# Two layers of a hybrid decoder trunk: a triangular inverse begun in 16x16 blocks on GpSimd, and the rotary row exchange done by transfers

## The reference, cut to what matters

```python
def rope(x, pos):                    # x1, x2: the two halves of a head's 64 channels
    return jnp.concatenate([x1 * cos - x2 * sin, x2 * cos + x1 * sin], -1).astype(x.dtype)

def delta_rule_scan(r, w, k, v, kk, a):
    def step(S, inp):
        r_t, w_t, k_t, v_t, kk_t, a_t = inp
        sa = jnp.einsum('bhvk,bhk->bhv', S, -kk_t)
        S = S * w_t[:, :, None, :] + sa[..., None] * (kk_t * a_t)[:, :, None, :] + v_t[..., None] * k_t[:, :, None, :]
        return S, jnp.einsum('bhvk,bhk->bhv', S, r_t)
```

## Time and profile before

| | |
|---|---|
| time, median of 3 runs | 1683.96 us (1683.74 to 1685.42) |
| the profiled execution, span from first to last instruction | 1682.6 us |
| PE (TensorE) busy | 1656.3 us, 98% |
| DVE (VectorE) busy | 1273.1 us, 76% |
| ACT (ScalarE) busy | 1001.9 us, 60% |
| POOL (GpSimd) busy | 2.9 us, 0% |
| traffic of HBM over the span | 244 GB/s |

### The profile page before, as it was taken

How to read it: one execution, slowest core, us unless ns; L and a number is a source line. 1 busy time by engine, 2 the same in 40 slices (tenths; PEclk the granted TensorE clock), 3 DMA queues, 4 the chain that set the end, 5 groups by cost and what they waited for, 6 DMA issues and landing times.

```text
span 1682.6 us, 27509 instructions
## 1 busy us (share of the span) xinstructions
PE 1656.3 (98%) x10650; PEld 1402.5 (83%) x10650; DVE 1273.1 (76%) x1226; ACT 1001.9 (60%) x968; POOL 2.9 (0%) x12
## 2 busy tenths in 40 slices
PE   9999999999999999999999999999999999999997
PEld 8988788778887998978888888888888888888885
DVE  5766775664446668496478899898988889898987
ACT  6554463454444645444446777777776777777775
POOL 0000000000000000000000000000000000000000
PEclk9999999999999999999998999999999999999999
DMA  9433333556564543334376999999999999998993
GB/s 295 137 116 126 125 126 101 204 166 199 175 199 150 188 144 109 113 125 127 101 255 236 364 353 384 325 373 330 393 336 373 364 335 394 328 367 322 392 374 143
DMA packets 216185, 411.04 MB, mean 244 GB/s; under 512 B 9376, under 2 KB 83488, under 8 KB 215584
## 3 DMA queue, kind: packets, MB, share of 16 engines
q1 hardware_dynamic: 213840, 400.97, 67.5%
q10 hardware_dynamic: 2256, 8.82, 1.4%
HBM read 407.66 MB, written 2.10 MB: 244 GB/s over the span
## 4 chain that ended last, share of the span: by engine, by line
PE 93%; DVE 4%; issue 1%; ACT 1%; DMA 0%; SPq 0%; DVEq 0%; ACTq 0%
PE W L503 20%; PE W L505 19%; PE W L504 19%; PE Y L503 7%; PE Y L504 7%; PE Y L505 7%; PE Y L796 4%; PE W L701 1%; DVE w_lo L1801 1%; PE Y L701 1%; PE Y L783 1%; PE E L708 0%; DMA raw<-w_in 0%; PE Y L1072 0%; PE Y L1073 0%
## 5 line engine op out<-in xcount | busy, mean ns | idle before, releaser
L503 PE MATMUL W<-w_lo,x_hi 128*128 128x512 f32 (+1 forms) x1168 | 452.8, 388 | 1.5 <-DVE x_lo L2115 0.9
L505 PE MATMUL W<-w_hi,x_hi 128*128 128x512 f32 (+1 forms) x1168 | 442.2, 379 | 0.0
L504 PE MATMUL W<-w_hi,x_lo 128*128 128x512 f32 (+1 forms) x1168 | 441.5, 378 | 0.0
L1801 DVE TENSOR_TENSOR w_lo<-raw,w_hi 128x2048 fp32r<-128x2048 f32 x112 | 256.5, 2291 | 174.0 <-ACT w_hi L1292 172.7
L1808 DVE TENSOR_TENSOR w_lo<-raw,w_hi 128x2048 fp32r<-128x2048 f32 x144 | 329.6, 2289 | 45.6 <-ACT w_hi L1298 45.6
L1298 ACT ACTIVATE w_hi<-raw 128x2048 fp32r<-128x2048 f32 x144 | 276.1, 1917 | 72.6 <-PE Y L505 40.0
L1808 DVE TENSOR_TENSOR w_lo<-raw_more,w_hi 128x2048 fp32r<-128x2048 f32 x120 | 275.0, 2291 | 28.3 <-ACT w_hi L1298 27.6
L1298 ACT ACTIVATE w_hi<-raw_more 128x2048 fp32r<-128x2048 f32 x120 | 230.5, 1921 | 64.8 <-PE W L505 42.0
L1292 ACT ACTIVATE w_hi<-raw 128x2048 fp32r<-128x2048 f32 x112 | 214.2, 1913 | 81.6 <-PE W L505 47.8
L503 PEld LDWEIGHTS W<-w_lo,x_hi 128*128 128x128 f32 x1168 | 219.9, 188 | 45.0 <-issue 4.5
L505 PEld LDWEIGHTS W<-w_hi,x_hi 128*128 128x128 f32 x1168 | 219.7, 188 | 42.0
(11 more groups left out here) (332 smaller groups left out, 1853.3 us busy)
## 6 DMA issues: line engine op xcount, KB each, us to landing
raw<-w_in SPq DMA_DIRECT2D x123, 512.0 KB, 4.6
raw<-moe_gate SPq DMA_DIRECT2D x48, 1024.0 KB, 6.4
raw<-moe_up SPq DMA_DIRECT2D x48, 1024.0 KB, 7.0
...
```

Source lines behind the costliest of these rows:

```text
L503: nc.tensor.matmul(out_ap, lhs[0], rhs[1], start=start, stop=False)
L504: nc.tensor.matmul(out_ap, lhs[1], rhs[0], start=False, stop=False)
L505: return nc.tensor.matmul(out_ap, lhs[0], rhs[0], start=False, stop=stop)
L1801: V.tensor_tensor(w_lo[u % 3][:], raw[u % 3][:], w_hi[u % 3][:].bitcast(F32), ALU.subtract)\
```

## The change

The first four levels (0 to 3) of the inverse are no longer doubled on PE. The 64x64 blocks hold 64 diagonal blocks of 16x16 per pass, and each is inverted by itself. `pick` (DVE) multiplies `ac` by a mask and sums it into `diag` (128x8x16). `solve` (GpSimd) then moves `diag` to HBM (1024 runs of 64 bytes), loads it with one 16x16 matrix in each of 64 partitions (64 runs of 1 KB), runs 14 rank-one updates of two instructions each and one `memset`, stores the result (64 runs) and loads it back in rows as `solved` (1024 runs). Each step waits for the one before. `place` (DVE) spreads `solved` into `xt`. Levels 4, 5 and 6 stay as they were. The rotary exchange is done by `swap` (GpSimd): four transfers of 32 partitions (64 KB each) per `rope`, SBUF to SBUF, and the sign is put into the sine table once. The steps move in `TIMELINE`: in the first pass levels 4 to 6 and all of `cg`, `cu`, `cy`, `mean`, `scaled` stand one unit later than before, in the second pass `invert` half a unit later and level 4 earlier, and ropes 0 and 1 stand one unit earlier, rope 3 half a unit. `scores` of the second pass stands one unit later.

```diff
+BASE = 4
+BS, NB = 1 << BASE, HD >> BASE
+NM = 8 * 2 * NB
+STEPS = TOP - BASE + 1
+SOLVED = 2 * (BS - 2) + 2
...
-    ("masks", 0), ("front", "conv", 2), ("back", "conv", 2), ("invert", 0), ("shift", 3),
-    ("front", "conv", 3), ("mx", 0, 1), ("back", "conv", 3), ("dx", 0, 1), ("lora_w", 1), ("rate_w", 1), ("shift", 4),
-    ("front", "conv", 4), ("mx", 0, 2), ("back", "conv", 4), ("dx", 0, 2), ("lora_a", 1), ("rate_a", 1), ("ksq", 1),
-    ("decay", 1),
-    ("front", "conv", 5), ("mx", 0, 3), ("exps", 1), ("back", "conv", 5), ("dx", 0, 3), ("ss", 1), ("knorm", 1), ("shift", 5),
-    ("front", "gate0", 0), ("mx", 0, 4), ("back", "gate0", 0), ("dx", 0, 4), ("spread", 1), ("kk", 1), ("conv", 0),
-    ("front", "gate0", 1), ("mx", 0, 5), ("back", "gate0", 1), ("dx", 0, 5), ("conv", 1),
-    ("front", "gate0", 2), ("mx", 0, 6), ("osplit", 0, 0), ("osplit", 0, 1), ("back", "gate0", 2), ("dx", 0, 6), ("prep", 1),
...
-    ("front", "qkv", 3), ("scaled", 0), ("bonus", 1), ("back", "qkv", 3), ("rope", 0), ("scores", 1, 0),
-    ("front", "qkv", 4), ("scores", 1, 1), ("compact", 1), ("back", "qkv", 4), ("rope", 1),
-    ("front", "qkv", 5), ("rope", 2), ("back", "qkv", 5),
-    ("front", "branch0", 0), ("rope", 3), ("back", "branch0", 0), ("att_scores", 0),
+    ("pick", 0), ("front", "conv", 2), ("back", "conv", 2), ("shift", 3),
+    ("front", "conv", 3), ("back", "conv", 3), ("lora_w", 1), ("rate_w", 1), ("shift", 4),
+    ("front", "conv", 4), ("back", "conv", 4), ("lora_a", 1), ("rate_a", 1), ("ksq", 1), ("decay", 1),
+    ("front", "conv", 5), ("exps", 1), ("back", "conv", 5), ("ss", 1), ("knorm", 1), ("shift", 5),
+    ("front", "gate0", 0), ("place", 0), ("back", "gate0", 0), ("invert", 0), ("spread", 1), ("kk", 1), ("conv", 0),
+    ("front", "gate0", 1), ("mx", 0, 4), ("back", "gate0", 1), ("dx", 0, 4), ("conv", 1),
+    ("front", "gate0", 2), ("mx", 0, 5), ("osplit", 0, 0), ("osplit", 0, 1), ("back", "gate0", 2), ("dx", 0, 5), ("prep", 1),
+    ("front", "gate0", 3), ("mx", 0, 6), ("back", "gate0", 3), ("dx", 0, 6),
+    ("front", "qkv", 0), ("cg", 0, 0), ("back", "qkv", 0), ("cu", 0, 0),
+    ("front", "qkv", 1), ("cy", 0, 0), ("back", "qkv", 1), ("cg", 0, 1),
+    ("front", "qkv", 2), ("cu", 0, 1), ("back", "qkv", 2), ("cy", 0, 1), ("yrow", 0), ("decayed", 1), ("rope", 0),
+    ("front", "qkv", 3), ("mean", 0), ("back", "qkv", 3), ("var", 0), ("tok", 1), ("rope", 1),
+    ("front", "qkv", 4), ("scaled", 0), ("bonus", 1), ("back", "qkv", 4), ("scores", 1, 0),
+    ("front", "qkv", 5), ("scores", 1, 1), ("compact", 1), ("rope", 2), ("back", "qkv", 5), ("rope", 3),
+    ("front", "branch0", 0), ("back", "branch0", 0), ("att_scores", 0),
...
-    ("front", "gate1", 2), ("att_out", 0), ("back", "gate1", 2), ("att_out", 1), ("masks", 1),
-    ("front", "gate1", 3), ("invert", 1), ("mx", 1, 1), ("dx", 1, 1), ("back", "gate1", 3), ("mx", 1, 2), ("dx", 1, 2),
-    ("front", "branch1", 0), ("mx", 1, 3), ("dx", 1, 3), ("back", "branch1", 0), ("mx", 1, 4), ("dx", 1, 4),
-    ("front", "branch1", 1), ("mx", 1, 5), ("dx", 1, 5), ("mx", 1, 6), ("dx", 1, 6),
+    ("front", "gate1", 2), ("att_out", 0), ("back", "gate1", 2), ("att_out", 1),
+    ("front", "gate1", 3), ("place", 1), ("back", "gate1", 3), ("invert", 1), ("mx", 1, 4),
+    ("front", "branch1", 0), ("dx", 1, 4), ("back", "branch1", 0), ("mx", 1, 5), ("dx", 1, 5),
+    ("front", "branch1", 1), ("mx", 1, 6), ("dx", 1, 6),
...
+        blocks_in, blocks_out = (nc.dram_tensor(name, (8, P, BS), F32, kind="Internal").ap() for name in ("blocks_in", "blocks_out"))
...
+        own_blocks = cm[:, 1, :]
+        def by_row(ap):
+            return ap.rearrange("u j t -> j u t")
+        def by_block(ap):
+            return ap.rearrange("u (b j) t -> (u b) (j t)", j=BS)
...
+        SWAPPED = (t4[:], t1[:], t2[:], fin2)
+        QUARTERS = [slice(a, a + HD // 2) for a in range(0, P, HD // 2)]
...
-            def rope(l, s):
-                wait_jobs(pe, l * MIX_JOBS + JOB0["qkv"] + s + 1)
-                if s:
-                    pe.wait_ge(sem("rope_ready"), 4 * l + s)
-                else:
-                    pe.wait_ge(sem("tok_ready"), 2 * l + 2)
-                nc.tensor.matmul(E[:], rot, share[:, 2 * s:2 * s + 2, :].rearrange("p m t -> p (m t)"),
-                                 start=True, stop=True).then_inc(sem("rot_done"), 1)
...
+            def moved(n, leg):
+                pool.wait_ge(sem("blocks_moved"), 16 * (4 * n + leg))
+            def solve(l, p):
+                n = 2 * l + p
+                made = SOLVED * n + 1
+                pool.wait_ge(sem("blocks_made"), made)
+                pool.dma_start(by_row(blocks_in), diag[:]).then_inc(sem("blocks_moved"), 16)
+                moved(n, 1)
+                pool.dma_start(own[:].rearrange("p j t -> p (j t)"), by_block(blocks_in)).then_inc(sem("blocks_moved"), 16)
+                moved(n, 2)
+                for m in range(1, BS - 1):
+                    rest = BS - 1 - m
+                    grown = step[:, 0:m, 0:rest]
+                    nc.gpsimd.tensor_tensor(grown, own[:, 0:m, m].unsqueeze(2).to_broadcast([NM, m, rest]),
+                                            own[:, m, m + 1:BS].unsqueeze(1).to_broadcast([NM, m, rest]), ALU.mult)\
+                        .then_inc(sem("blocks_made"), 1)
+                    pool.wait_ge(sem("blocks_made"), made + 2 * m - 1)
+                    nc.gpsimd.tensor_tensor(own[:, 0:m, m + 1:BS], own[:, 0:m, m + 1:BS], grown, ALU.add)\
+                        .then_inc(sem("blocks_made"), 1)
+                    pool.wait_ge(sem("blocks_made"), made + 2 * m)
+                nc.gpsimd.memset(own[:].rearrange("p j t -> p (j t)")[:, ::BS + 1], 1.0).then_inc(sem("blocks_made"), 1)
+                pool.wait_ge(sem("blocks_made"), SOLVED * (n + 1))
+                pool.dma_start(by_block(blocks_out), own[:].rearrange("p j t -> p (j t)")).then_inc(sem("blocks_moved"), 16)
+                moved(n, 3)
+                pool.dma_start(solved[:], by_row(blocks_out)).then_inc(sem("blocks_moved"), 16)
+            def swap(l, s):
+                wait_jobs(pool, l * MIX_JOBS + JOB0["qkv"] + s + 1)
+                if s == 3:
+                    pool.wait_ge(sem("var_done"), 2 * l + 1)
+                elif s:
+                    pool.wait_ge(sem("decayed_ready"), 2 * l + 2)
+                else:
+                    pool.wait_ge(sem("prep_ready"), 2 * l + 2)
+                for i, to in enumerate(QUARTERS):
+                    pool.dma_start(SWAPPED[s][to], share[QUARTERS[i ^ 1], 2 * s:2 * s + 2, :]).then_inc(sem("swapped"), 16)
+                pool.wait_ge(sem("swapped"), 64 * (4 * l + s + 1))
+            for l in range(L):
+                solve(l, 0)
+                corner(l, 0)
+                for s in range(4):
+                    swap(l, s)
+                solve(l, 1)
+                corner(l, 1)
...
+            def pick(l, p):
+                n = 2 * l + p
+                if n == 0:
+                    for v, other in ((1, 0), (1, 2), (1, 3), (1, TOP)):
+                        link(V.tensor_tensor(own_blocks, cm[:, v, :], cm[:, other, :], ALU.add))
                 dve.wait_ge(sem("ac_ready"), n + 1)
+                picked = t3[:].rearrange("p m (u t) -> p (m u) t", t=HD)
+                link(V.tensor_tensor(picked, ac[:], own_blocks.unsqueeze(1).to_broadcast([P, 8, HD]), ALU.mult))
+                V.reduce_sum(diag[:], picked.rearrange("p u (b t) -> p u t b", b=NB), AX.X).then_inc(sem("blocks_made"), 1)
+            def place(l, p):
+                n = 2 * l + p
                 for c in range(NT):
+                    link(mask_level(BASE, c))
+                dve.wait_ge(sem("blocks_moved"), 16 * (4 * n + 4))
+                blocks = own_blocks.rearrange("p (b t) -> p b t", b=NB).unsqueeze(1).to_broadcast([P, 4, NB, BS])
                 for c in range(NT):
                     mine = slice(4 * c, 4 * c + 4)
+                    mark(V.tensor_tensor(xt[:, mine, 0, :].rearrange("p u (b t) -> p u b t", b=NB),
+                                         solved[:, mine, :].unsqueeze(2).to_broadcast([P, 4, NB, BS]), blocks, ALU.mult),
+                         "xt_ready", 2 * (STEPS + 1) * n + c + 1)
...
-                dve.wait_ge(sem("rot_done"), 4 * l + s + 1)
-                V.tensor_tensor(t4[:], tiles(E[:]), sin, ALU.mult)
+                other = SWAPPED[s]
+                if l == 0 and s == 0:
+                    dve.wait_ge(sem("cst_full"), 96)
+                    for quarter in QUARTERS[0::2]:
+                        last = V.tensor_scalar(cst[quarter, C_SIN:C_END], cst[quarter, C_SIN:C_END], -1.0, None, ALU.mult)
+                    link(last)
+                dve.wait_ge(sem("swapped"), 64 * (4 * l + s + 1))
+                V.tensor_tensor(other, other, sin, ALU.mult)
                 link(V.tensor_tensor(src, src, cos, ALU.mult))
-                mark(V.tensor_tensor(src, t4[:], src, ALU.add), "rope_ready", 4 * l + s + 1)
```

(37 more changed lines are left out.)

26 lines of the change are left out of this document (11 added, 15 removed).

## The result

The changed kernel takes 1671.9 us (median of 4 runs, 1671.4 to 1673.2) beside 1683.9 for the kernel before on the same chip: ratio 0.9928, 95% interval 0.9917 to 0.9940. The gain is 12.0 us where I forecast 32.3. The profiled execution has a span of 1669.6 us.

The account below looks back on a forecast made before the run. PE's instruction stream was taken as the bound. Sparing PE matmuls and waits gains 49.3 us, less 2.0 for first-pass waits and 15.0 for second-pass stops: 32.3 off 1684.0, forecast 1652 us, range 1636 to 1676 for 8 in 10.

Parts of the forecast that it names:

- The number of matmuls: On PE: 1152 fewer rows of 64x64, and no 128x512 rows into `E` from `share`.
- C: Chain from `pick` to `place`: four transfers at 2.7 us, 29 GpSimd instructions at 0.36, 21 us; bounds 13 and 40.
- rival (a): The chain stops PE in the second pass only, C from 16 to 26 us; 1640 to 1662 us; chance 0.50.
- The cover there: Second pass, from `pick`'s end until PE wants the result at `invert`: 15.0 us, so C is 6.0 us longer.
- 1.5 us of clock for a stop: PE's rows run at half clock after idling: 1.5 us added to each stop of more than 2 us.
- The ropes' 9.3 us: Rope matmuls taken off PE: 0.9 us a rope, 3.6 a layer; plus 2.1 us of waits for rope 3.
- Rival (c): The chain outlasts both passes' covers, C of 27 to 31 us; 1674 us at C = 29; chance 0.16.
- the fight between the engines: GpSimd stands still for 5 to 7 us of DVE's `w_lo` and `o_lo`, second cover: about 1665 us; about one in three.
- The lower price in the prediction: The Trainium skill's estimate for a GpSimd transfer of 64 KB: 2.15 us, making the time some 4 us less.
- place behind w_lo: First pass on DVE: `w_lo` starts 2.9 us into PE's unit, so PE waits 1.0 us at `invert`, twice 2.0.
- the 0.8 us at the scores: PE's four waits for the scores, 0.8 us, should go because no rope stands between the two steps of scores.
- rival (b): The chain fits its covers, C of 15 us or less: 47.3 us less, 1637 us; chance 0.18.

Follow-up runs that it names:

- keep_clock: The changed kernel with 20 matmuls of zeros put into PE's stop before `invert` of the second pass: 1668.8 us, ratio 0.9911.
- pe_ropes: The changed kernel with the four ropes of a layer on TensorE again, at the new places or within half a unit: 1681.2 us, ratio 0.9982.
- quiet_chain: The changed kernel with `w_lo` of gate1's last unit moved on DVE behind `place` of the second pass: 1669.6 us, ratio 0.9916.
- no_chain: The changed kernel without the whole of `solve`, so `place` multiplies zeros and the output differs: 1646.2 us, ratio 0.9784.
- late_low: The changed kernel with one number different: `w_lo` stands in the back half of qkv 4 on DVE instead of qkv 3: 1671.0 us, ratio 0.9918.
- transfers_only: The changed kernel without the 28 `tensor_tensor` instructions of `solve`, transfers and `memset` kept, so the output differs: 1645.4 us, ratio 0.9775.

## Why the prediction fell short

**What was right.** The number of matmuls, and that the chain would stop PE in the second pass. C of 24.9 us is inside rival (a), but (a) had PE stop in the second pass only, and its prices give 1659.5 us for this C; the other 12 us are the second and third point below. The cover there: PE wants the result at 235.7, 15.15 us after `pick`, less the 0.57 from `place` to PE 14.6; I had 15.0. The first: 25.8, I had 26.5. 1.5 us of clock for a stop, near the 1.1 and 1.4 of keep_clock. The ropes' 9.3 us agree with pe_ropes in size only, and that is partly luck, since 2.1 of them were another wait. Rival (c) named the fight between the engines, and it is there, at 1.9 us and not 5 to 7: of the three `w_lo` inside the second cover two ran while GpSimd issued its transfers or waited for them, and the `o_lo` at 230.66, with one input from PSUM, held no row.

**The step that failed first: C.** "I take 2.7" a transfer and 0.36 an instruction gave 21 us; it is 24.9 and 25.1 in the second pass, 29.6 and 30.0 in the first. An undisturbed instruction with its gap takes 0.35, so this price held; 1.9 us are the one row held by `w_lo` (quiet_chain), 2.1 the transfers. "DMA is busy for 35 to 39% here, so it is nearest the first" took an average over 67 us: three of the first pass's four transfers ran beside shares of 0.47 to 0.75. The lower price in the prediction, 2.15 us a transfer, was nearly met once in four (2.23), in the stop itself. The second stop became 10.3 and 10.5 us instead of 6.0: 8.8 us lost in the two layers.

**The second: place behind w_lo.** "In the trace it starts 2.9 us after PE begins this unit" took a distance between two engines from the old order, where PE still had level 3 to do over ACT's run. I had subtracted these matmuls from PE and let ACT and DVE come forward with it. It is 3.0 without the chain (no_chain) and 3.84 and 4.16 with it: 6.0 us lost, and the clock behind it, for which I had put nothing. In no_chain the first pass's stop of 3.0 us is followed by half the clock in layer 0 and not in layer 1, and from the first scores to the second layer 0 takes 1.6 us longer (115.8 against 114.2), so I estimate some 3 us for two stops.

**The third: a wait that I didn't look for.** I took out the 0.8 us at the scores and put nothing in. `scaled` had moved one unit on, the number that lets `w_lo` stand behind it had not, and PE waits 1.8 us in each layer: 3.6. By late_low that number is the cause of this wait, but most of the lateness comes back at the attention scores, so it was to be had back only in small part.

**The sum.** 32.3 - 8.8 - 6.0 - 3 - 3.6 = 10.9 beside 12.0 measured. The 3 is an estimate, the other terms are PE's waits. The floor closes as well: 47.3 of rival (b), less 4.0 for the first pass (3.0 instead of 1.0, twice), 3.6 for the scores and some 3 for the clock, is 36.7; no_chain gained 37.1.

**What stays open.** The same 3.0-us stop lost the clock once and kept it once in no_chain and lost it twice in transfers_only, and no run here tells why. Nor did I separate by a run whether the load on the DMA engines makes the same transfer take 2.2 us in the second pass and 4.2 in the first.
